# The expert outputs of a mixture layer go back to their tokens by indirect DMA stores in place of one-hot matmuls

## The chip, the core and the metric

The kernel runs on one core of a Trainium2 chip. The metric is the device time of one launch, in microseconds; the times given are medians over runs. Its engines are called as the profile calls them: PE (TensorE, with PEld for its weight loads), DVE (VectorE), ACT (ScalarE), POOL (GpSimd) and SP (SyncE, which here only issues DMAs). "PEq", "SPq" and so on are the sequencers of these engines.

## The reference, cut to what matters

A trunk of two layers over 256 tokens of width 1024. Only the last block matters here, an expert layer that sends each token to its two best of eight experts:

```python
top_v, top_i = lax.top_k(logits, 2)
top_w = jax.nn.softmax(top_v, axis=-1)
combine = jnp.sum(jax.nn.one_hot(top_i, 8) * top_w[..., None], axis=-2)
out = jnp.zeros_like(h)
for e in range(8):                       # w_gate[e], w_up[e]: 1024 x 3584, w_down[e]: 3584 x 1024
    out = out + combine[..., e:e + 1] * swiglu(h, w_gate[e], w_up[e], w_down[e])
x = x + g2 * out                         # then a final RMSNorm with shift and scale
```

All is float32. The eight experts' weights are 352 MB of the 500 MB that the kernel reads.

## The kernel before, in words

The work before the expert layer (retention, a dense SwiGLU, attention, the router) isn't touched. The expert layer runs from about 644 us to the end.

**Passes.** Expert e is one pass: 128 slots hold the tokens that chose it (a ninth to eleventh pass would serve experts with over 128 tokens; in the profiled run there are 8 passes, numbered 0 to 7 here). A pass has 7 chunks of 512 hidden columns, and a chunk has 6 units of weights of 1 MB: two of gate, two of up, two of down. Pass 0 and the last chunk of pass 7 are written out; passes 1 to 7 run in a hardware loop (`Fori`, L2050 on PE), whose body first ends pass w-1 (its last chunk and its last down step), and begins pass w. That stretch is called the turn from one pass to the next.

**One unit.** SP waits until PE has used up the slot of the ring (6 slots, semaphore `w_used`, L412) and loads 1 MB in two DMAs (L416). ACT casts it to the high part (`high_e`, L906), DVE subtracts to get the low part (`low_e`, L1432, two operands in SBUF: `stage` and `hi`), and PE multiplies three times, high by high, high by low and low by high (`three`, L1656 to L1658): 12 matmuls of 128x128 by 128x512 a unit. The order of the work on each engine is written out by hand; each engine runs ahead of PE as far as the ring allows.

**Tokens of a pass.** DVE builds one-hot matrices of slots by comparing a row of indices with each token's position (`choose`, L1477): `pick` for the pass whose output is to be put back, `pick_next` for the next pass. PE turns `pick` by two transposes (L1968) and multiplies `pick_next` by the token numbers, which gives the token of each slot of the next pass (L1970). ACT copies both out (`take_put`, L940). POOL makes an integer of the token numbers (L603) and fetches these rows of the hidden state by an indirect DMA into `grow` (L607). Some 80 us later PE transposes `grow` (L1978), for the next pass.

**Output of a pass.** The down product of pass w-1 lies in PSUM banks 4 and 5. ACT copies its high part (`take_down`, L954), DVE makes the low part (`low_down`, L1520), and PE scatters the 128 slots back to 256 tokens by 8 matmuls with the turned `pick`:

```python
def scatter(n):
    pe.wait_ge(dn_done, n)
    pe.wait_ge(put_done, n)
    for t in range(TT):
        for n in range(2):
            cols = slice(n * CB, (n + 1) * CB)
            mm(bank[:, (6, 4)[t] + n, :], put[:, t * P:(t + 1) * P], dn_hi[:, cols], start=True, stop=False)
            ins = mm(bank[:, (6, 4)[t] + n, :], put[:, t * P:(t + 1) * P], dn_lo[:, cols], start=False, stop=True)
        ins.then_inc(scat, 1)
```

DVE adds the result, weighted, to the sum `moe` (`add`, L1528, twice a pass). PE's first down step of pass w waits for that (L2064), since it writes banks 4 and 5 again.

**The end.** After the last unit, `take_down`, `low_down` and `scatter` run once more for the last pass (L2073), DVE adds it to the residual (L1621, L1625), and the final norm and the store of the output follow.

Of the kernel before, what the change touches and what calls it, by code (L numbers as in the profile page):

```python
# [8 lines left out]
P = 128  # L9
D = 1024  # L10
SEQ = 256
# [9 lines left out]
E = 8  # L21
# [33 lines left out]
SLOTS = 128  # L55
N_TAB = 16
# [25 lines left out]
def shape_constants():  # L82
# [16 lines left out]
    c[:, C_EPS + 1:C_EPS + 1 + TT] = np.arange(SEQ).reshape(TT, P).T  # L99
    j = np.arange(P)[:, None]  # L100
# [9 lines left out]
def encoder(nc, x, c, l0_ada_w, l0_ada_b, l0_norm1_g, l0_norm2_g, l0_ret_w_in, l0_ret_decay_logit,  # L110
# [5 lines left out]
    with ctx:  # L116
# [95 lines left out]
        gidx = at("gidx", [1], R + 52 * KW, I32)  # L212
        grow = at("grow", [D], R + 16 * KW)
        eaT2_hi = at("eaT2_hi", [4, SLOTS], R + 20 * KW, F32R)
# [22 lines left out]
        h_dram = nc.dram_tensor("h_rows", [SEQ, D], F32, kind="Internal").ap()  # L237

# [122 lines left out]
        grow_free = sem("grow_free")  # L361

# [36 lines left out]
        def _(sp):  # L399
# [6 lines left out]
            sp.sem_inc(moe_add, TT)  # L406
            sp.sem_inc(scat, 1)
# [113 lines left out]
        def _(pool):  # L521
# [77 lines left out]
            passes = pool.value_load(meta[0:1, 2 * N_TAB:2 * N_TAB + 1], min_val=E, max_val=E + 3)  # L599
            with pool.Fori(1, passes) as w:  # L600
# [4 lines left out]
                pool.wait_ge(g_tr, w)  # L605
                pool.sem_inc(grow_free, 1)
                nc.gpsimd.indirect_dma_start(out=grow[:, :], out_offset=None, in_=h_dram[:, :],  # L607
                                             in_offset=bass.IndirectOffsetOnAxis(ap=gidx[:, 0:1].bitcast(U32), axis=0)
                                             ).then_inc(grow_in, 16)


        @block.scalar
        def _(act):
# [322 lines left out]
            def take_put(w, first=False):  # L936
                act.wait_ge(put_tr, w + 1)
                if not first:
                    act.wait_ge(gidx_done, w)
                nc.scalar.copy(put[:, 0:SEQ + 1], bank[:, 3, 0:SEQ + 1]).then_inc(put_done, 1)  # L940
# [35 lines left out]
            take_put(0, True)  # L976
# [5 lines left out]
            with act.Fori(1, passes) as w:  # L982
# [15 lines left out]
                take_down(w, m + (RING + U_MOE + 4))  # L998
# [4 lines left out]
                take_put(w)  # L1003
# [5 lines left out]
            high_e(U_END - 1, m, o)  # L1009
            e_high_act(o + (E * N_EC - 1), eaT2_hi)  # L1010
            take_down(extra + E, m + (RING + U_END))
# [1086 lines left out]
```

## Time and profile before

| what | value |
|---|---|
| median of 3 runs (lowest, highest) | 1654.36 us (1654.05, 1655.42) |
| the profiled execution's own time | 1656.82 us |
| its span | 1654.6 us |
| PE busy | 1563.3 us, 94% of the span |
| DVE busy | 1362.7 us, 82% |
| ACT busy | 978.9 us, 59% |
| POOL busy | 151.7 us, 9% |
| moved by DMA | 503.16 MB |

The busy time of an engine is the union of its instructions' times. Matmuls overlap each other in the records: one is listed with 0.40 us, but the next starts 0.23 us after it, and it is this distance that counts. All times "at x us" are from the start of the span.

### The profile page before, as it was taken

How to read it: one execution, taken by the hardware profiler on the slowest of the kernel's cores; microseconds unless marked ns; L12 is line 12 of the kernel's file. 1: busy time of each engine (PE TensorE's matmuls, PEld its weight loads, DVE VectorE, ACT ScalarE, POOL GpSimd, SP SyncE). 2: the span in 40 equal slices, each digit the busy share in tenths (PEclk: the TensorE clock that was granted, in tenths of full speed). 3: DMA queues.
4: the chain of work that ended last, by engine and by line, in shares of the span. 5: the costliest groups of instructions: out<-in, count | busy, mean ns of one | idle time of the engine just before them, and what ended most of it. 6: DMA issues, size and time to landing. Idle time of an engine off the chain costs nothing.

```text
span 1654.6 us, 20642 instructions
## 1 busy us (share of the span) xinstructions
PE 1563.3 (94%) x6848; PEld 1248.5 (75%) x6848; DVE 1362.7 (82%) x1076; ACT 978.9 (59%) x790; POOL 151.7 (9%) x146
## 2 busy tenths in 40 slices
PE   5999779899997689999999999999999999999996
PEld 4677547677776568887888888888888888888885
DVE  6799478877767767888888888888888888888987
ACT  3444523433433636677777677677667667677763
POOL 0399400000002001000000000000000000000000
PEclk8999989999998898999999999999999999999998
DMA  9799319698894325999999999999999999999993
GB/s 340 281 346 354 118 38 360 234 304 268 296 323 131 121 67 203 378 365 347 357 368 353 356 366 353 356 369 352 356 367 353 356 367 353 355 366 355 343 368 119
DMA packets 237789, 503.16 MB, mean 304 GB/s; under 512 B 15725, under 2 KB 38381, under 8 KB 237625
## 3 DMA queue, kind: packets, MB, share of 16 engines
q1 hardware_dynamic: 234704, 491.50, 82.8%
q0 software_dynamic: 2464, 9.09, 1.6%
q10 hardware_dynamic: 586, 2.11, 0.3%
q8 instruction: 21, 0.34, 0.1%
q14 instruction: 14, 0.11, 0.0%
HBM read 500.54 MB, written 2.11 MB: 304 GB/s over the span
## 4 chain that ended last, share of the span: by engine, by line
PE 90%; DVE 6%; ACT 1%; issue 1%; DMA 1%; SPq 0%; DVEq 0%; ACTq 0%
PE bank L1656 27%; PE bank L1657 27%; PE bank L1658 27%; PE bank L1984 1%; PE bank L1637 1%; PE bank L1746 1%; DVE lo L1032 1%; DMA xs<-in_x 1%; PE bank L1651 0%; DVE hs L1070 0%; PE bank L1642 0%; PE bank L1864 0%; PE bank L2008 0%; SPq L435 0%; PE bank L2007 0%
## 5 line engine op out<-in xcount | busy, mean ns | idle before, releaser
L1432 DVE TENSOR_TENSOR lo<-stage,hi 128x2048 fp32r<-128x2048 f32 x168 | 383.7, 2287 | 53.0 <-ACT hi L906 52.7
L906 ACT CAST hi<-stage 128x2048 fp32r<-128x2048 f32 x168 | 321.4, 1913 | 134.0 <-DMA stage<-in_l_moe_w_up 119.0
L1657 PE MATMUL bank<-lo,hg_hi 128*128 128x512 f32 x896 | 354.3, 395 | 0.0
L625 ACT CAST hi<-stage 128x2048 fp32r<-128x2048 f32 x75 | 143.2, 1912 | 146.9 <-PE bank L1658 75.0
L1032 DVE TENSOR_TENSOR lo<-stage,hi 128x2048 fp32r<-128x2048 f32 x75 | 173.2, 2312 | 42.0 <-ACT hi L625 35.7
L1657 PEld LDWEIGHTS bank<-lo,hg_hi 128*128 128x128 f32 x896 | 168.8, 188 | 37.6
L1656 PE MATMUL bank<-hi,hT_hi 128*128 128x512 f32 x416 | 172.8, 415 | 10.0 <-DVE lo L1032 8.5
L1656 PE MATMUL bank<-hi,hg_hi 128*128 128x512 f32 x452 | 180.0, 398 | 0.2 <-issue 0.2
L1658 PE MATMUL bank<-hi,hg_lo 128*128 128x512 f32 x452 | 179.0, 396 | 0.0
L1657 PE MATMUL bank<-lo,eaT_hi 128*128 128x512 f32 x448 | 177.7, 397 | 0.0
L1657 PE MATMUL bank<-lo,hT_hi 128*128 128x512 f32 x416 | 167.5, 403 | 0.0
L1658 PE MATMUL bank<-hi,hT_lo 128*128 128x512 f32 x416 | 167.3, 402 | 0.0
L1432 DVE TENSOR_TENSOR lo<-stage,hi_h 128x2048 fp32r<-128x2048 f32 x56 | 128.3, 2291 | 40.2 <-ACT hi_h L906 40.0
L906 ACT CAST hi_r<-stage 128x2048 fp32r<-128x2048 f32 x56 | 106.9, 1908 | 61.1 <-DMA stage<-in_l_moe_w_gate 59.7
L1044 DVE SCALAR_TENSOR_TENSOR ada_acc<-ada_w,cact,ada_acc 128x512 f32<-128x512 f32 x168 | 131.8, 785 | 7.4 <-DVE ada_acc L1044 2.3
L1432 DVE TENSOR_TENSOR lo<-stage,hi_m 128x2048 fp32r<-128x2048 f32 x56 | 128.2, 2290 | 10.4 <-ACT hi_m L906 10.0
L1432 DVE TENSOR_TENSOR lo<-stage,hi_r 128x2048 fp32r<-128x2048 f32 x56 | 128.1, 2288 | 9.2 <-ACT hi_r L906 8.5
L906 ACT CAST hi_h<-stage 128x2048 fp32r<-128x2048 f32 x56 | 107.1, 1912 | 41.1 <-DMA stage<-in_l_moe_w_gate 40.7
L906 ACT CAST hi_m<-stage 128x2048 fp32r<-128x2048 f32 x56 | 107.2, 1914 | 40.3 <-DMA stage<-in_l_moe_w_down 40.3
L1656 PEld LDWEIGHTS bank<-hi,hT_hi 128*128 128x128 f32 x416 | 80.3, 193 | 32.5 <-DVE lo L1032 6.4
L1658 PEld LDWEIGHTS bank<-hi,hg_lo 128*128 128x128 f32 x452 | 85.1, 188 | 20.9
L1656 PEld LDWEIGHTS bank<-hi,hg_hi 128*128 128x128 f32 x452 | 85.1, 188 | 20.7 <-issue 0.4
(291 smaller groups left out, 2703.2 us busy)
## 6 DMA issues: line engine op xcount, KB each, us to landing
stage<-in_l_moe_w_gate SPq DMA_DIRECT2D x224, 512.0 KB, 4.5
stage<-in_l_moe_w_up SPq DMA_DIRECT2D x224, 512.0 KB, 4.9
stage<-in_l_moe_w_down SPq DMA_DIRECT2D x224, 512.0 KB, 4.5
ada_w<-in_l_ada_w SPq DMA_DIRECT2D x40, 1024.0 KB, 5.3
stage<-in_l_ret_w_in SPq DMA_DIRECT2D x48, 512.0 KB, 7.5
stage<-in_l_ffn_w_gate SPq DMA_DIRECT2D x22, 512.0 KB, 7.6
stage<-in_l_ffn_w_up SPq DMA_DIRECT2D x22, 512.0 KB, 8.6
stage<-in_l_ffn_w_down SPq DMA_DIRECT2D x22, 512.0 KB, 7.6
```

The lines of the kernel that those rows point to most:

```text
L625: nc.scalar.copy(hi[:, b % HRING, :], stage[:, b % RING, :]).then_inc(hi_done, 1)
L906: nc.scalar.copy(hi_e(b), stage[:, b % RING, :]).then_inc(hi_done, 1)
L1032: nc.vector.tensor_tensor(lo[:, b % RING, :], stage[:, b % RING, :], hi[:, b % HRING, :].bitcast(F32), ALU.subtract).then_inc(lo_done, 1)
L1044: ins = nc.vector.scalar_tensor_tensor(out=acc, in0=ada_w[:, half, j, :], scalar=cact[:, k:k + 1], in1=acc if k else ada_b[:, :], op0=ALU. ...
L1432: nc.vector.tensor_tensor(lo[:, b % RING, :], stage[:, b % RING, :], hi_e(b).bitcast(F32), ALU.subtract).then_inc(lo_done, 1)
L1637: mm(bank[:, 3, :], ones, ada_acc[:, c % 2, :], start=True, stop=True).then_inc(a_sum, 1)
L1656: mm(dst_ap, a_hi, w_hi, start=first, stop=False)
L1657: mm(dst_ap, a_hi, w_lo, start=False, stop=False)
L1658: return mm(dst_ap, a_lo, w_hi, start=False, stop=last)
L1746: ins = mm(bank[:, (7, 2)[t], :], dec[:, h % 2, jt * SEQ + t * P:jt * SEQ + (t + 1) * P], proj[:, 4 + h, jt, :], start=(jt == 0), stop=(jt ...
L1984: ins = nc.tensor.transpose(bank[:, 2, k * P:(k + 1) * P], eact[:, k * P:(k + 1) * P], ident)
```

## The change

Every pass but the last no longer scatters by matmuls. ACT copies the down product once, at full width, into `yout`; POOL stores its 128 rows by an indirect DMA to an internal DRAM tensor `y_rows` of 512 rows: row n is token n's result from its first expert, row 256 + n that from its second. Slots without a token get an index over the bound and are skipped. The rows are set to zero first (two DMAs of 1 MB from the zeroed `moe`). The index of each row comes from a matmul of the one-hot matrix with a table `tokv` of 9 columns (`index_rows`), which takes the place of the transposes and of the one-column product. After the last turn POOL reads `y_rows` back (four DMAs of 512 KB), multiplies both halves by their weights and adds them into `moe`; DVE's last stretch waits for that. The last pass still scatters by matmuls. The diff, cut to its core (new semaphores and their declarations are left out):

```diff
+        y_dram = nc.dram_tensor("y_rows", [2 * SEQ, D], F32, kind="Internal").ap()
...
             nc.gpsimd.memset(moe[:, :, :], 0.0).then_inc(m_zero, 1)
+            yv = y_dram.rearrange("(r t p) d -> r p t d", r=2, p=P)
+            pool.wait_ge(m_zero, 1)
+            for r in range(2):
+                pool.dma_start(yv[r], moe[:, :, :]).then_inc(y_zero, 16)
...
             with pool.Fori(1, passes) as w:
+                e = pool.value_load(meta[0:1, bass.ds(w, 1)], min_val=0, max_val=E - 1)
                 pool.wait_ge(put_done, w)
+                pool.wait_ge(sidx_done, w)
                 pool.sem_inc(put_seen, 1)
-                nc.gpsimd.tensor_copy(gidx[:, 0:1], put[:, SEQ:SEQ + 1].bitcast(F32)).then_inc(gidx_done, 1)
+                nc.gpsimd.tensor_copy(snext[:, 0:1], ix[:, bass.ds(e, 1)]).then_inc(snext_done, 1)
+                nc.gpsimd.tensor_copy(gidx[:, 0:1], ix[:, 8:9]).then_inc(gidx_done, 1)
...
                 nc.gpsimd.indirect_dma_start(out=grow[:, :], out_offset=None, in_=h_dram[:, :],
...
+                nc.gpsimd.tensor_scalar(snext[:, 0:1], snext[:, 0:1], float(NOWHERE), None, ALU.add).then_inc(snext_done, 1)
+                pool.wait_ge(dn_out, w)
+                pool.sem_inc(y_go, 1)
+                nc.gpsimd.indirect_dma_start(out=y_dram[:, :],
+                                             out_offset=bass.IndirectOffsetOnAxis(ap=sidx[:, 0:1].bitcast(U32), axis=0),
+                                             in_=yout[:, :], in_offset=None, bounds_check=2 * SEQ - 1, oob_is_err=False
+                                             ).then_inc(y_out, 16)
+                pool.wait_ge(y_out, w * 16)
+                pool.wait_ge(snext_done, w * 2)
+                pool.sem_inc(y_sent, 1)
+                nc.gpsimd.tensor_copy(sidx[:, 0:1], snext[:, 0:1]).then_inc(sidx_done, 1)
...
+            for t in range(TT):
+                pool.dma_start(moe[:, t, :], yv[0, :, t, :]).then_inc(y_in, 16)
+                pool.dma_start(ysec[t][:, :], yv[1, :, t, :]).then_inc(y_in, 16)
+            pool.wait_ge(y_in, 64)
+            for t in range(TT):
+                nc.gpsimd.tensor_scalar(moe[:, t, :], moe[:, t, :], rsm[:, t, 5, 2:3], None, ALU.mult)
+                link(nc.gpsimd.tensor_scalar(ysec[t][:, :], ysec[t][:, :], rsm[:, t, 5, 3:4], None, ALU.mult))
+                nc.gpsimd.tensor_tensor(moe[:, t, :], moe[:, t, :], ysec[t][:, :], ALU.add).then_inc(y_sum, 1)
...
+            def take_out(w, used):
+                act.wait_ge(w_used, used)
+                act.wait_ge(y_sent, w)
+                nc.scalar.copy(yout[:, :], bank[:, 4:6, :].rearrange("p b n -> p (b n)")).then_inc(dn_out, 1)
...
-                take_down(w, m + (RING + U_MOE + 4))
+                take_out(w, m + (RING + U_MOE + 4))
...
+            act.wait_ge(put_tr, extra + (E + 1))
+            nc.scalar.copy(put[:, 0:SEQ], bank[:, 3, 0:SEQ]).then_inc(put_done, 1)
...
             choose(pick_next, slice(1, 2)).then_inc(pick_done, 1)
+            for t in range(TT):
+                nc.vector.tensor_copy(tokv[:, t, 8:9], cst[:, C_EPS + 1 + t:C_EPS + 2 + t])
+                ins = nc.vector.tensor_scalar(tokv[:, t, 0:E], rsm[:, t, 7, :], float(SEQ), cst[:, C_EPS + 3 + t:C_EPS + 4 + t],
+                                              ALU.mult, ALU.add)
+            ins.then_inc(tokv_done, 1)
...
-                choose(pick, bass.ds(col, 1))
                 choose(pick_next, bass.ds(col_next, 1)).then_inc(pick_done, 1)
...
-                low_down(w)
                 low_e(b + 3, m)
                 e_low_act(o)
-                add((w * TT, w * TT + 1), bass.ds(before, 1))
...
+            def index_rows(w):
+                pe.wait_ge(pick_done, w + 2)
+                for t in range(TT):
+                    ins = mm(bank[:, 3, 0:9], pick_next[:, t, :].bitcast(F32), tokv[:, t, 0:9], start=(t == 0), stop=(t == TT - 1))
+                ins.then_inc(put_tr, 1)
...
                 e_half(U_MOE + 4, 0, m)
-                scatter(w)
-                turn_pick(w)
                 e_half(U_MOE + 4, 1, m)
-                pe.wait_ge(moe_add, w * TT + TT)
+                pe.wait_ge(put_done, w)
+                index_rows(w)
+                pe.wait_ge(dn_out, w)
                 e_down_step(U_MOE + 8, m, o, True, False)
...
+            pe.wait_ge(put_done, extra + E)
+            turn_pick(extra + (E + 2))
             e_gate_up(U_END - 8, m, o + (E * N_EC - 1))
...
-            scatter(passes)
+            scatter()
```

`yout` takes the place of `dn_hi` in SBUF, and the second halves are read into `grow` and `normg`. DVE's last stretch (L1610) waits for `y_sum` in place of `moe_add`, and makes the last `pick` there.

## Rows read from the trace of the kernel before

**Rows 1.** The page, part 2: busy tenths of PE in forty slices of the span
```profile
PE   5999779899997689999999999999999999999996
```

**Rows 2.** Window of one pass: from:to, each engine's busy us (instructions), granted clock, DMA share, GB/s
```profile
888.00:1012.00 124.00, 124.00 (x554) 100.41 (x553) 108.49 (x65) 88.74 (x60) 2.78 (x2) 1.00 0.98 359
```

**Rows 3.** Waits of PE in 657 to 1636 us; then of SP's queue: us, times, longest
```profile
PE bank L1656 <- issue: 0.5, 1, 0.5
...
SPq L416 <- PE bank L1658: 737.6, 359, 42.5
```

**Rows 4.** Timeline of PE at the first turn: start us, us, instruction (lines left out repeat the pattern)
```profile
785.01 0.40 PE L2007 MATMUL bank<-dn_hi,put 128*128 128x512 f32 x1
...
786.86 0.38 PE L1968 MATMUL bank<-cst,pick 128*128 128x128 f32 x2
787.08 0.50 PE L1970 MATMUL bank<-cst,pick_next 128*128 128x1 f32 x4
787.44 0.47 PE L1656 MATMUL bank<-hi,hg_hi 128*128 128x512 f32 x1
```

**Rows 5.** The tile `moe`: instructions, ns min/median/max, first and last start
```profile
L1528 DVE SCALAR_TENSOR_TENSOR moe<-bank,comb,moe x14: 1272/1276/1285, 786.5 to 1532.8; 128x1024 f32<-128x1024 f32 x14
```

**Rows 6.** Timelines of DVE and PE: when a unit's low part is made, and its first matmul, twice
```profile
701.78 2.29 DVE L1432 TENSOR_TENSOR lo<-stage,hi_h 128x2048 fp32r<-128x2048 f32 x1 [0.86 <-ACT hi_h L906]
708.62 0.48 PE L1656 MATMUL bank<-hi_h,hg_hi 128*128 128x512 f32 x1
788.84 2.28 DVE L1432 TENSOR_TENSOR lo<-stage,hi 128x2048 fp32r<-128x2048 f32 x1
793.14 0.39 PE L1656 MATMUL bank<-hi,eaT_hi 128*128 128x512 f32 x1
```

**Rows 7.** Windows right after a gather, columns as in rows 2
```profile
664.00:684.00 20.00, 20.00 (x90) 16.11 (x89) 17.60 (x10) 12.77 (x9) 0.00 (x0) 1.00 1.04 392
664.00:704.00 40.00, 40.00 (x177) 32.27 (x176) 35.77 (x20) 27.84 (x18) 0.00 (x0) 1.00 1.03 380
```

**Rows 8.** POOL's gather: the line, its landing, and the transposes that use it (first and last start)
```profile
L607 POOL DMA_INDIRECT grow<-h_rows,gidx x7: 1014/2592/2593, 659.5 to 1410.3; - x7
...
DMA to landing us min/median/max: 6.0/8.0/8.0
...
L1978 PE MATMUL bank<-cst,grow x56: 272/272/273, 743.2 to 1490.2; 128*128 128x128 f32 x56
```

**Rows 9.** Timelines of POOL and DVE at 200 us, then L1032 in 210 to 500 us
```profile
200.74 1.71 POOL L564 TENSOR_TENSOR proj<-proj,gn 128x512 f32<-128x512 f32 x1
201.25 3.35 DVE L1032 TENSOR_TENSOR lo<-stage,hi 128x2048 fp32r<-128x2048 f32 x1
L1032 DVE TENSOR_TENSOR lo<-stage,hi x40: 2279/2292/2295, 213.1 to 496.1; 128x2048 fp32r<-128x2048 f32 x40
```

**Rows 10.** POOL's elementwise work by line: ns min/median/max
```profile
L564 POOL TENSOR_TENSOR proj<-proj,gn x8: 1263/1372/3314, 196.2 to 208.1; 128x512 f32<-128x512 f32 x8
L596 POOL MEMSET moe<- x1: 1805/1805/1805, 630.6 to 630.6; 128x2048 f32 x1
```

**Rows 11.** The layer's start: a window (columns as in rows 2), then timelines of DVE and PE
```profile
633.00:647.00 14.00, 13.80 (x82) 13.10 (x81) 8.78 (x13) 7.99 (x6) 0.00 (x0) 0.77 0.00 1
655.65 0.69 DVE L1487 TENSOR_TENSOR eact<-bank,esil 128x512 f32<-128x512 f32 x1 [0.27 <-PE bank L1658]
656.39 0.66 PE L1984 MATMUL bank<-cst,eact 128*128 128x128 f32 x4 [0.23 <-DVE eact L1487]
```

**Rows 12.** The end: timelines of ACT, then of PE
```profile
1628.27 0.59 ACT L949 CAST eaT_hi<-bank 128x512 fp32r<-128x512 f32 x1 [2.00 <-PE bank L1984]
1639.09 0.51 PE L2007 MATMUL bank<-dn_hi,put 128*128 128x512 f32 x1 [2.43 <-DVE dn_lo L1520]
1639.66 0.62 PE L2007 MATMUL bank<-dn_hi,put 128*128 128x512 f32 x1
1640.08 0.63 PE L2008 MATMUL bank<-dn_lo,put 128*128 128x512 f32 x1
```

More of the change, by code:

```diff
@@ L55 @@
 SLOTS = 128
+NOWHERE = 4096
 N_TAB = 16
@@ L212, in encoder @@
         gidx = at("gidx", [1], R + 52 * KW, I32)
+        sidx = at("sidx", [1], R + 52 * KW + 8, I32)
+        snext = at("snext", [1], R + 52 * KW + 16)
+        ix = at("ix", [32], R + 52 * KW + 32)
+        tokv = at("tokv", [TT, 16], R + 52 * KW + 64)
+        yout = at("yout", [D], R + 42 * KW)
         grow = at("grow", [D], R + 16 * KW)
+        ysec = [grow, normg]
         eaT2_hi = at("eaT2_hi", [4, SLOTS], R + 20 * KW, F32R)
@@ L361, in encoder @@
         grow_free = sem("grow_free")
+        y_zero = sem("y_zero")
+        y_out = sem("y_out")
+        y_sent = sem("y_sent")
+        y_go = sem("y_go")
+        y_in = sem("y_in")
+        y_sum = sem("y_sum")
+        dn_out = sem("dn_out")
+        snext_done = sem("snext_done")
+        sidx_done = sem("sidx_done")
+        tokv_done = sem("tokv_done")
         def in_unit(u):
@@ L405, in _ @@
             sp.sem_inc(proj_out, 3)
-            sp.sem_inc(moe_add, TT)
-            sp.sem_inc(scat, 1)
+            sp.sem_inc(y_sent, 1)
             sp.sem_inc(g_tr, 1)
@@ L934, in take_rows, with take_index @@
                 nc.scalar.copy(hg_hi[:, :, :], bank[:, 6:8, :].rearrange("p b (k n) -> p (b k) n", k=4)).then_inc(hg_hi_done, 1)
-            def take_put(w, first=False):
+            def take_index(w, first=False):
                 act.wait_ge(put_tr, w + 1)
-                if not first:
+                if first:
+                    nc.scalar.copy(ix[:, 0:24], bank[:, 3, 0:24]).then_inc(put_done, 1)
+                else:
                     act.wait_ge(gidx_done, w)
-                nc.scalar.copy(put[:, 0:SEQ + 1], bank[:, 3, 0:SEQ + 1]).then_inc(put_done, 1)
+                    act.wait_ge(snext_done, w * 2)
+                    nc.scalar.copy(ix[:, 0:9], bank[:, 3, 0:9]).then_inc(put_done, 1)
             def e_silu_step(n, used):
@@ L975, in _ @@
             e_high_act(0)
-            take_put(0, True)
+            take_index(0, True)
             high_e(U_MOE + 8)
@@ L1009, in _ @@
             high_e(U_END - 1, m, o)
+            act.wait_ge(put_tr, extra + (E + 1))
+            nc.scalar.copy(put[:, 0:SEQ], bank[:, 3, 0:SEQ]).then_inc(put_done, 1)
             e_high_act(o + (E * N_EC - 1), eaT2_hi)
+            act.wait_ge(y_sent, extra + E)
             take_down(extra + E, m + (RING + U_END))
@@ L1609, in _ @@
             m = mods[:, 1, 2]
-            dve.wait_ge(moe_add, passes * TT)
             for t in range(TT):
+                dve.wait_ge(y_sum, t + 1)
                 ins = nc.vector.tensor_tensor(moe[:, t, :], moe[:, t, :], m, ALU.mult)
@@ L1998, in e_down_step, with scatter @@
                         e_turn(between)
-            def scatter(n):
-                pe.wait_ge(dn_done, n)
-                pe.wait_ge(put_done, n)
+            def scatter():
+                pe.wait_ge(dn_done, 1)
+                pe.wait_ge(put_done, extra + (E + 1))
                 for t in range(TT):
@@ L2041, in _ @@
             e_half(U_MOE, 1, 0)
-            turn_pick(0)
+            pe.wait_ge(tokv_done, 1)
+            for t in range(TT):
+                mm(bank[:, 3, 16:24], pick[:, t, :].bitcast(F32), tokv[:, t, 0:E], start=(t == 0), stop=(t == TT - 1))
+            index_rows(0)
             e_turn(0)
```

39 lines of the change are left out of this document (20 added, 19 removed).

## The prediction

> **What bounds the kernel now.** I read the slices first. The last 24 of 40 show PE at 9 tenths nearly throughout [rows 1]: the expert layer. A window as long as a pass then says PE 124.00 us of 124.00, DVE 108.5, ACT 88.7, DMA share 0.98 at 359 GB/s [rows 2]. So two resources are nearly full, PE and the DMA, and the waits must say which one leads. PE waits 0.5 us in the whole layer, while SP's queue waits 737.6 us for PE to free a slot of the ring [rows 3]. PE leads: what it sheds is gained, as long as weights, ACT and DVE keep up. How far they are ahead is in rows 6. A low part is done at 701.78 + 2.29 = 704.07 us and used at 708.62, a lead of 4.5 us; after a turn, where DVE has extra work, it is 793.14 - 791.12 = 2.0 us.
>
> One turn lies between the first adds at 786.5 and the next; the last add starts at 1532.8, some 1.2 us after its pair's first, so six turns take 745.1 us, 124.2 us each [rows 5].
>
> **Part 1, PE in the turns.** The scatter starts at 785.01 us, the transposes at 786.86, the one-column product at 787.08, the next gate matmul at 787.44 [rows 4]: 2.43 us. What stays is a product of 9 columns in place of one, two instructions of the same kind; no row has 9 columns, so I bound it by 0.36 us (one column, 787.44 - 787.08) and 0.6 us (with the 0.22 us that two 128-column transposes take on top). I take 0.36, as 9 columns are nearest to one. The saving is 2.07 us a turn, on the path since PE never waits; seven turns give **14.5 us** (12.8 at the other bound). A pass becomes 122.1 us.
>
> **Part 2, DVE and ACT in the turns.** DVE loses two adds of 1.28 us [rows 5], a low part of half a unit's width (half of the 2.28 us in rows 6) and one pair of comparisons, some 4 us; ACT copies 9 columns instead of 257. No PE wait ends on either now, so this is 0 us; it only lifts the lead above its low of 2.0 us.
>
> **Part 3, the stores and the gather.** A store is 128 rows of 4 KB at most, 0.52 MB, about half of it on average (512 results over 8 experts are 64 rows each). The nearest row is the gather of the same size: 2.6 us on POOL, landing in at most 8 us [rows 8]. POOL now holds the gather back until the store has landed: issued near 785 us, landed near 795, gather issued near 797 and landed near 805. The first gather, issued at 659.5 us, is used at 743.2 [rows 8]; 42 us before the scatter of its turn (785.01). With turns 124.2 us apart the next rows are wanted at about 867 us, so 60 us are left. `yout` is wanted again a pass later. ACT's wait for `y_sent`, behind which its casts are queued, costs nothing for the same reason. On the DMA the cost is bytes: 42 units of 1.049 MB and a gather make 44.6 MB a pass now (359 GB/s over 124.2 us, as rows 2 have it), 44.8 to 45.1 MB then, over 122.1 us: 367 to 369 GB/s. After the first gather the DMA moved 392 GB/s for 20 us and 380 for 40 us with PE never idle [rows 7]. So the weights can keep up: 0 us; if they can't, that is the second rival.
>
> **Part 4, the start.** The zeros are 2.1 MB, sent from about 633 us. From 633 to 647 us the DMA moves 1 GB/s, since the ring is full [rows 11]; at 392 GB/s they need 5.4 us. Hidden. DVE makes `tokv` by four operations on at most 8 columns before its `eact` at 655.65 us, where it had 0.27 us to spare, and PE already waits for that [rows 11]. No row shows so narrow a one; each costs more than nothing and less than the 0.69 us of `eact` with 512 columns. I take 0.14 us each, near the low end as they are narrow: 0.55 - 0.27 = **0.3 us** (0 to 2.5).
>
> **Part 5, reading back.** After turn 7 (about 1520 us) POOL loads 2.1 MB beside the weights: 5.4 us of the DMA at 392 GB/s. Against it stands the lead of 4.5 us [rows 6].
>
> Then POOL combines: four scalings and two additions of 128x1024. This is where I expect a loss. At 200.74 us POOL starts a tensor_tensor that reads SBUF; DVE's subtraction at 201.25, in the very shape of the expert layer, takes 3.35 us where 40 others take 2.29 [rows 9]. The 1.06 us extra are the rest of POOL's operation (it ends at 202.45), and POOL's longest operation there, 3.31 us against a least of 1.26 [rows 10], is the reverse. So such operations exclude each other, and DVE, 87% busy mostly with these subtractions, alternates with POOL. A POOL addition of 512 columns takes 1.26 us, so 1024 take about 2.35 (double is 2.53, of which I take off a little, since part of the 1.26 is a fixed cost). A scaling isn't in the trace: the memset writes 2048 columns in 1.81 us [rows 10], 0.9 us for 1024, the lower end; 2.35 us is the upper end. I take 1.0, since with one input it is nearest to the memset. The sum held against DVE is 4 x 1.0 + 2 x 2.35 = 8.7 us, less the 12.5% that DVE idles [rows 2] over some 25 us, 3 us: 5.7 us. Readback and combine together are 5.4 + 5.7 = 11.1 us late; if they share one lead of 4.5 us, PE stops 6.6 us; if the lead is won back between them, 0.9 + 1.2 = 2.1 us. I take the middle, **4.4 us**. The ends of this term: 0, if DVE's idle time and its lifted lead cover all, and 12 us, with scalings of 2.35 us (14.1 us held) and a clock that falls while PE starves.
>
> The Trainium skill (SBUF — State Buffer, Who interferes with whom) says that a DVE instruction with two SBUF inputs contends with a GpSimd instruction that reads SBUF, and that the second to issue fully blocks. Rows 9 agree, by 3.35 against 2.29 us.
>
> **Part 6, the end.** Two transposes before the last chunk: **0.2 us**. ACT's copy of `put`, shorter than the 0.59 us of 512 columns, falls into the 2.00 us that it idles before 1628 us [rows 12]. DVE's wait for `y_sum` stands at that point too, and is met some 60 us early. The last scatter and the norm don't change.
>
> **Sum.** -14.5 + 0.3 + 4.4 + 0.2 = **-9.6 us**. The profiled execution took 1656.8 us (1654.6 us of span and 2.2 around it) and would take 1647.2. The runs' median is 2.5 us lower, 1654.4, so I predict **1644.8 us** there, with a range of its own of 1642 to 1648.
>
> **The rivals.**
> *The lead covers the combine.* No stall: -14.5 + 0.5 = -14.0, 1640.4 us. For it: DVE is relieved of some 4 us just before. Against it: 11 us of disturbance lie within some 30. Chance 0.15.
>
> *The DMA is the bound (slower).* Were 359 GB/s [rows 2] what the DMA can hold on average, a pass with its store would take 45.1 MB / 359 = 125.6 us instead of 124.2, seven of them +9.8 us, and the readback 2.1 MB / 359 = 5.8 us more: +15.6, 1670 us. It decides below 369 GB/s, and loses outright below 363 (45.1 MB in 124.2 us). For it: every pass shows 359. Against it: the queue waits for PE [rows 3], and 392 and 380 GB/s were moved in rows 7. Chance 0.06.
>
> The Trainium skill (DMA: Bandwidth & Descriptors, Specifications) gives a limit from device memory of about 358 GB/s for a core; by that rule this rival would be right. Rows 7 exceed it by a tenth. The same skill (HBM Reference, Specifications (TRN2)) has a core that streams alone at about 425 GB/s, which rows 7 do not contradict.
>
> *The combine starves PE.* Scalings as slow as additions, or a reading back that is slower than its bytes: -14.5 + 0.5 + 11 = -3, 1651.4 us. After an idle of 2.43 us PE's matmuls follow each other at 0.42 us (1639.66 to 1640.08) instead of 0.23 [rows 12], so stalls of that length cost again until the clock is back. Chance 0.13.
>
> *It does not do what it says.* If a store, with its check of the bound, took over 70 us, the gather would be late and each turn would wait. At 8 us for the gather this is far off. Chance 0.02, about no change.
>
> **How the numbers follow.** The forecast has 0.64. A measurement of this kernel can tell 0.2%, 3.3 us, from no change: faster means under 1651.1, slower over 1657.7. Faster: 0.64 + 0.15, nearly half of the third rival, and those runs of the DMA case that only eat a part: 0.87. Same: 0.07. Slower: 0.06. The range takes in the first rival and most of the third: 1639.5 to 1651.
>
> **What would show it.** Right: PE's timeline at 785 us goes from gate to up matmuls without a gap, and two matmuls of 128x9 stand before the down step; turns 122.1 us apart; PE idle 2 to 7 us in all between 1520 and 1560 us, put down to DVE's low parts, with subtractions of 3 to 4.5 us beside POOL's scalings. Each scaling near 1.0 us. DMA at 367 to 369 GB/s in a pass. Wrong: PE waiting for DVE or DMA in every turn (the DMA bound), turns over 123 us apart, or POOL's gather issued more than 40 us after the store.

## The result and the profile after

Side by side on one chip, the changed kernel takes 1643.93 us (median of 5 runs, 1642.87 to 1647.75) and the kernel before 1655.42 us (5 runs, 1654.05 to 1656.88). The ratio is 0.9936, with a 95% interval of 0.9922 to 0.9950. That is 0.6% and clear of no change, so faster by the bound of 0.2% that the forecast set. I had forecast 1644.8 us, and faster with 0.87.

The page of the profiled execution (1642.87 us, span 1641.0 us), parts 1 and 2:

```profile
PE 1545.9 (94%) x6782; PEld 1234.3 (75%) x6782; DVE 1341.8 (82%) x1047; ACT 976.7 (60%) x791; POOL 198.3 (12%) x189
POOL 0399500000002001100100100000000000000600
```

PE's slices in the expert layer are at 9 tenths, as in [rows 1]. POOL's last busy slice, a 6 that is third from the end, is the combination of the results.

**The turn.** The timeline of PE at the first turn, to be read against [rows 4]:

```profile
787.29 0.39 PE L1715 MATMUL bank<-hi,hg_lo 128*128 128x512 f32 x1
787.52 0.51 PE L2025 MATMUL bank<-tokv,pick_next 128*128 128x9 f32 x4
787.88 0.48 PE L1713 MATMUL bank<-hi,eaT_hi 128*128 128x512 f32 x1
```

The scatter and the transposes are gone. The product of 9 columns takes 787.88 - 787.52 = 0.36 us, the value taken for it.

**A pass.** A window of the length of a pass, columns as in [rows 2]:

```profile
888.00:1010.00 122.00, 122.00 (x545) 98.86 (x544) 104.78 (x60) 88.83 (x60) 4.74 (x6) 1.00 1.00 367
```

PE is busy all the time, and the DMA delivers 367 GB/s where it delivered 359 [rows 2].

**The waits** of 640 to 1500 us in the trace after (us, times, longest), then PE's of 1515 to 1625 us:

```profile
POOL sidx L650 <- DMA y_rows<-yout,sidx: 28.7, 6, 5.1
ACT ix L995 <- PE bank L2025: 23.0, 6, 4.6
...
PE bank L1713 <- DVE lo L1496: 2.5, 2, 1.3
```

The second line is new. ACT copies the indices of the next pass (`ix`), and since the change these come from the product that stands behind the two up units. ACT waits 2.6 to 4.6 us for it at every turn, with its casts of weights queued behind. The last line is the only wait of PE between 1515 and 1625 us.

**Where the time went.** The layer has 42 units a pass, 336 in all, numbered from 0. The time of PE's first matmul of a unit cuts the span into stretches. "Lead" is the time from the end of a unit's low part on DVE to its first matmul, as in [rows 6].

| stretch | before | after | difference |
|---|---|---|---|
| start to the first expert matmul | 644.12 | 641.18 | -2.9 |
| to unit 295, in the last pass (six turns) | 871.80 | 859.21 | -12.6 |
| unit 295 to 335 (seventh turn, reading back) | 117.77 | 119.70 | +1.9 |
| unit 335 to the end | 20.89 | 20.89 | 0.0 |
| sum (span) | 1654.6 | 1641.0 | -13.6 |

The first row isn't the change's. It is TensorE's clock while the router is computed. The windows of before, then of after (granted clock third from the end):

```profile
627.00:644.00 17.00, 16.92 (x107) 16.73 (x107) 9.37 (x27) 11.63 (x10) 1.80 (x1) 0.70 0.26 101
```

```profile
627.00:641.00 14.00, 13.98 (x109) 13.74 (x108) 9.51 (x27) 11.76 (x10) 3.23 (x3) 0.88 0.73 281
```

PE does about the same work at a mean of 0.70 there and of 0.88 here. Over the runs of the changed kernel and its variants the first expert matmul lies between 638.4 and 644.3 us, so this is scatter (e3_no_readback, which starts the layer at 644.26, shows the slow clock there as well). It is also why single spans are compared by stretches below. The change's own part is -12.6 + 1.9 = -10.7 us.

A turn saves 2.07 us: from a unit to the same unit of the next pass it is 124.23 us before and 122.15 after, the difference before rounding 2.07. Six turns make -12.4 of the second row, and the first turn saved 0.2 more. In the third row the seventh turn's -2.07 and the 0.2 of the pick ahead of the last chunk would leave -1.9; it shows +1.9, so the stall behind the seventh turn is **+3.8 us**. The experiments are about that stall.

**The stall in the trace.** POOL after the last store, in the trace after:

```profile
1513.11 1.48 POOL L643 DMA_INDIRECT y_rows<-yout,sidx  x1 [109.68 <-ACT yout L1015]
1518.90 0.21 POOL L650 CAST sidx<-snext 128x1 int32<-128x1 f32 x1 [4.31 <-DMA y_rows<-yout,sidx]
1519.61 0.58 POOL L655 DMA_DIRECT2D moe<-y_rows  x1 [0.51 <-issue]
...
1521.26 0.54 POOL L656 DMA_DIRECT2D normg<-y_rows  x1
1532.25 2.87 POOL L659 TENSOR_SCALAR moe<-moe,rsm 128x1024 f32<-128x1024 f32 x1 [10.45 <-DMA normg<-y_rows]
1535.10 4.25 POOL L660 TENSOR_SCALAR grow<-grow,rsm 128x1024 f32<-128x1024 f32 x1
1539.43 2.58 POOL L661 TENSOR_TENSOR moe<-moe,grow 128x1024 f32<-128x1024 f32 x1
1542.00 7.00 POOL L659 TENSOR_SCALAR moe<-moe,rsm 128x1024 f32<-128x1024 f32 x1
1548.98 5.27 POOL L660 TENSOR_SCALAR normg<-normg,rsm 128x1024 f32<-128x1024 f32 x1
1554.33 2.58 POOL L661 TENSOR_TENSOR moe<-moe,normg 128x1024 f32<-128x1024 f32 x1
```

DVE beside it, same trace:

```profile
1534.34 2.29 DVE L1496 TENSOR_TENSOR lo<-stage,hi 128x2048 fp32r<-128x2048 f32 x1 [3.83 <-ACT hi L958]
1537.14 2.61 DVE L1496 TENSOR_TENSOR lo<-stage,hi 128x2048 fp32r<-128x2048 f32 x1
1539.67 4.49 DVE L1496 TENSOR_TENSOR lo<-stage,hi_m 128x2048 fp32r<-128x2048 f32 x1
...
1546.89 2.52 DVE L1496 TENSOR_TENSOR lo<-stage,hi_r 128x2048 fp32r<-128x2048 f32 x1
1549.33 5.32 DVE L1496 TENSOR_TENSOR lo<-stage,hi 128x2048 fp32r<-128x2048 f32 x2
1555.17 3.89 DVE L1496 TENSOR_TENSOR lo<-stage,hi 128x2048 fp32r<-128x2048 f32 x1
```

And ACT, then PE, where the two disturbances reach them:

```profile
1521.09 0.17 ACT L995 COPY ix<-bank 128x9 f32<-128x9 f32 x1 [4.13 <-PE bank L2025]
1532.39 1.91 ACT L958 CAST hi<-stage 128x2048 fp32r<-128x2048 f32 x1 [5.61 <-DMA stage<-in_l_moe_w_up]
```

```profile
1536.68 0.50 PE L1713 MATMUL bank<-hi,hg_hi 128*128 128x512 f32 x1 [1.18 <-DVE lo L1496]
1544.21 0.50 PE L1713 MATMUL bank<-hi_m,eaT_hi 128*128 128x512 f32 x1 [1.34 <-DVE lo L1496]
```

The reader sees two stalls with two causes. The reads go out in one burst at 1519.6 us, and the next up unit reaches ACT 5.61 us after ACT is free for it; PE stops at unit 307. Then the subtraction at 1539.67 takes 4.49 us, with POOL's first addition (1539.43 to 1542.01) ahead of it; PE stops at unit 309. The two waits listed are 2.5 us of the 3.8. Set unit by unit against a trace without the stall (e3 below), PE is later by 1.34 us at unit 307, 0.31 at 308, 1.60 at 309, and 0.5 in all at 310, 314 and 315, in gaps too short for the list of waits.

### The profile page after: what moved, and what is told of

Its sections match the earlier page's. It is cut to its first block, busy times and chain, and to the rows that moved or that the text cites. A ratio compares the mean times of both kernels' runs of the same rounds, so it can differ in the third digit from the quotient of the medians.

```text
span 1641.0 us, 20506 instructions
## 1 busy us (share of the span) xinstructions
PE 1545.9 (94%) x6782; PEld 1234.3 (75%) x6782; DVE 1341.8 (82%) x1047; ACT 976.7 (60%) x791; POOL 198.3 (12%) x189
## 4 chain that ended last, share of the span: by engine, by line
PE 89%; DVE 6%; ACT 1%; DMA 1%; issue 1%; SPq 0%; DVEq 0%; ACTq 0%
PE bank L1713 27%; PE bank L1714 27%; PE bank L1715 27%; PE bank L2045 1%; PE bank L1694 1%; PE bank L1803 1%; DVE lo L1096 1%; DMA xs<-in_x 1%; DMA stage<-in_l_moe_w_up 1%; PE bank L1708 1%; DVE hs L1134 0%; PE bank L1921 0%; DVE lo L1496 0%; SPq L453 0%; PE bank L2039 0%
## 5 line engine op out<-in xcount | busy, mean ns | idle before, releaser
L643 POOL DMA_INDIRECT y_rows<-yout,sidx x7 | 10.3, 1469 | 774.1 <-ACT yout L1015 774.1
```

## The experiments

Theory A: the lead is used up by ACT's new wait, by the bytes read back, and by POOL's arithmetic, which keeps DVE off. Theory B: the extra DMA traffic alone makes the stall. Theory C: the DMA is the bound throughout. The column "295 to 335" is taken from the profiled execution of each; the change without any disturbance shows 115.92 there. Each is one trace, and the stop at unit 307 alone, read against e3, lies between 0.9 and 1.5 us over seven traces that read back in one burst (e5, e2, e6, after_again, e1, the changed kernel, e8; 2.0 in after_third), so differences of half a microsecond between stretches say little.

| run | 295 to 335, us | last pass's least lead | median us | ratio to before, 95% |
|---|---|---|---|---|
| changed kernel | 119.70 | 0.05 | 1643.93 | 0.9936 [0.9922, 0.9950] |
| e1_index_early | 119.74 | 0.05 | 1644.09 | 0.9946 [0.9930, 0.9961] |
| e2_no_combine | 117.11 | 0.05 | 1641.91 | 0.9923 [0.9909, 0.9938] |
| e3_no_readback | 115.92 | 1.37 | 1638.78 | 0.9908 [0.9892, 0.9924] |
| e4_store_twice | 120.25 | 0.05 | 1645.39 | 0.9951 [0.9936, 0.9966] |
| e5_scale_more | 118.80 | 0.05 | 1642.42 | 0.9927 [0.9914, 0.9941] |
| e6_act_combine | 117.47 | 0.06 | 1642.09 | 0.9920 [0.9902, 0.9937] |
| e8_act_scale | 117.79 | 0.06 | 1645.67 | 0.9947 [0.9930, 0.9963] |
| after_again | 119.70 | 0.06 | 1642.83 | 0.9935 [0.9920, 0.9950] |
| e9_paced_act | 117.43 | 1.05 | 1641.07 | 0.9920 [0.9907, 0.9934] |
| e10_paced_pool | 119.74 | 0.06 | 1646.29 | 0.9946 [0.9932, 0.9959] |
| after_third | 122.66 | 0.05 | 1644.18 | 0.9935 [0.9921, 0.9948] |
| e11_paced_early | 115.93 | 1.07 | 1640.95 | 0.9920 [0.9902, 0.9938] |

The expectations speak of unit 300 to 335. Where the index product is early, it falls ahead of unit 300 and not behind it, which shortens that stretch by some 0.3 us (105.25 becomes 104.92 in e1) and gains nothing; from unit 295 on the columns compare.

**e1_index_early.** PE makes the index product before the second half.

```
+                pe.wait_ge(put_done, w)
+                index_rows(w)
                 e_half(U_MOE + 4, 1, m)
-                pe.wait_ge(put_done, w)
-                index_rows(w)
                 pe.wait_ge(dn_out, w)
```

> Edit: PE makes the index rows between the two halves of the chunk, where the turned one-hot matrix was made before, and no longer after the second half. Theory A (ACT's copy of the index waits some 4 us for PE at each turn, and this eats the lead of DVE over PE, so that at the last turn the reading back and the combine find a lead of 1.4 us): ACT's wait before its copy of ix falls from 27 us in all to under 3, the least lead at the turns rises from 1.4 us to 2.5 or more, and PE's stall after the last turn falls from 3.8 us to 1 to 2, so the time falls by 2 to 3 us against the changed kernel (some 1641.5). Rival B (the low lead comes from the store's bytes on the DMA, not from ACT's wait): the wait goes, the leads stay under 2 us, the stall and the time stay within 1 us.

ACT's wait for `ix` vanished from the list of waits, and the least leads behind the first six turns rose from 1.37 to between 1.85 and 3.05 us, so rival B's leads under 2 us came at one turn of the six. The stall did not fall either, as theory A had it: the stretch is 119.74. The timeline of ACT in this run:

```profile
1517.26 0.16 ACT L995 COPY ix<-bank 128x9 f32<-128x9 f32 x1
1524.69 1.91 ACT L958 CAST hi<-stage 128x2048 fp32r<-128x2048 f32 x1 [0.85 <-DMA stage<-in_l_moe_w_up]
1532.61 1.91 ACT L958 CAST hi<-stage 128x2048 fp32r<-128x2048 f32 x1 [6.00 <-DMA stage<-in_l_moe_w_up]
```

ACT is no longer late, but the unit behind the reads is still cast at 1532.61 (1532.39 in the changed kernel), which is 31.98 us behind unit 295 here and 32.00 there. Its landing is set by the DMA, whatever ACT did before. So the new wait is real and costs nothing here: this step of theory A falls.

**e2_no_combine** leaves out the weighting and adding of the stored results (they are read back), **e3_no_readback** the reading back as well.

```
-            for t in range(TT):
-                nc.gpsimd.tensor_scalar(moe[:, t, :], moe[:, t, :], rsm[:, t, 5, 2:3], None, ALU.mult)
...
+            pool.sem_inc(y_sum, TT)
```

> Edit: POOL's four scalings and two additions at the end are left out (so the experts' outputs are not weighted and the second halves are not added), the reading back stays. Theory A (POOL's operations and DVE's subtractions exclude each other): DVE's subtractions after the last turn are all 2.29 us long, and PE's stall there falls from 3.8 us to under 1.5; the time is 2.5 to 4 us under that of the changed kernel, some 1640. Rival B (the stall is the DMA's, by the 2.1 MB read back): the stall stays at 3 us or more.

> Edit: neither reading back nor combine (the outputs of all experts but the last are left out of the result). Both theories: no stall of PE in the expert layer, turns 122.1 us apart, and the floor of this design: the span's part from the first expert matmul to the end is 3.8 us shorter than in the changed kernel, about 1640. Against the run without the combine it prices the reading back alone: theory A 0 to 1.5 us, rival B 3 us or more.

Without the arithmetic the stretch is 117.11, without the reads 115.92. So the reads alone cost 117.11 - 115.92 = **1.2 us**, and the arithmetic on top of them 119.70 - 117.11 = **2.6 us** (0.2 of it at unit 307, where no subtraction was long yet). No subtraction is long in e2, as expected; its median is 2.0 us under the changed kernel's, where 2.5 to 4 were expected. ACT in e3 at the unit that stands behind the reads in the others:

```profile
1530.56 1.91 ACT L951 CAST hi<-stage 128x2048 fp32r<-128x2048 f32 x1 [0.75 <-DMA stage<-in_l_moe_w_up]
```

Counted from unit 295 (at 1500.39 us in the changed kernel, 1503.41 in e3), this cast starts at 32.00 and at 27.15: the burst makes it 4.9 us late. PE came 1.34 us late for it, so 3.5 us were covered: 2.6 by the lead at unit 307 (2.63 in e3), and 0.9 because DVE took the cast up at once instead of 1.0 us later.

**e4_store_twice** stores the rows of every pass a second time, to another DRAM tensor.

```
+                nc.gpsimd.indirect_dma_start(out=y_more[:, :],
+                                             out_offset=bass.IndirectOffsetOnAxis(ap=sidx[:, 0:1].bitcast(U32), axis=0),
+                                             in_=yout[:, :], in_offset=None, bounds_check=2 * SEQ - 1, oob_is_err=False
+                                             ).then_inc(y_out, 16)
```

> Edit: each pass stores its rows twice, the second time into another DRAM tensor, and POOL waits for both (no output changes). Theory A (PE paces the layer and the DMA has room): turns stay 122.1 us apart, the gather is issued 1.5 to 3 us later and still some 50 us early, the time is that of the changed kernel within 1.5 us. Rival C (the DMA is the bound, at 359 to 369 GB/s): 0.26 to 0.5 MB more a pass make turns 0.7 to 1.4 us longer, 5 to 10 us in all, some 1650 to 1654.

The turns stay at 122.15 us; only the last pass takes 0.55 us more. Theory C falls: the DMA still has room for another store in every pass. Counted from the first expert matmul POOL issued the gather 4.2 us later than in the changed kernel (1.5 to 3 were expected); its rows are used at 865.9 us, and no wait of PE came of it:

```profile
784.66 2.79 POOL L648 DMA_INDIRECT y_more<-yout,sidx  x1 [0.30 <-issue]
794.20 1.27 POOL L655 CAST sidx<-snext 128x1 int32<-128x1 f32 x1 [6.76 <-DMA y_more<-yout,sidx]
796.92 2.19 POOL L638 DMA_INDIRECT grow<-h_rows,gidx  x1 [0.91 <-POOL gidx L633]
```

**e5_scale_more** makes each scaling twice, so the combination uses the squares of the weights.

```
+                for _ in range(2):
+                    link(nc.gpsimd.tensor_scalar(moe[:, t, :], moe[:, t, :], rsm[:, t, 5, 2:3], None, ALU.mult))
+                    link(nc.gpsimd.tensor_scalar(ysec[t][:, :], ysec[t][:, :], rsm[:, t, 5, 3:4], None, ALU.mult))
```

> Edit: every scaling of the read-back results on POOL is made twice (so each result is multiplied by its weight squared), the additions stand as they are. Theory A (POOL's arithmetic holds DVE off and lengthens its subtractions, and the last lead is already gone when it starts): six long POOL instructions become ten, the stretch from unit 300 to 335 grows from 105.2 us by 1.5 to 4 us, more than five subtractions are long, time 1645.5 to 1648. Theory B (the stall is made by the DMAs of the reading back, not by arithmetic): the stretch stays at 105.2 within 0.4 us and the time at 1644. A third way, that only the additions exclude DVE (two inputs) and the scalings do not: no change either, but the scalings' own rows would then last 1 us each when no subtraction runs.

None of the three came. Twice the scalings made the stall *shorter*, 118.80 against 119.70. Half of the difference, 0.45 us, stands at unit 307 (PE 0.89 us late instead of 1.34), where no subtraction is long in either trace, so that half comes from the reads and not from the scalings. The rows of POOL bear on the other half, and on why nothing grew:

```profile
1539.66 5.14 POOL L660 TENSOR_SCALAR moe<-moe,rsm 128x1024 f32<-128x1024 f32 x1
1544.89 3.04 POOL L661 TENSOR_SCALAR grow<-grow,rsm 128x1024 f32<-128x1024 f32 x1
1548.02 2.60 POOL L662 TENSOR_TENSOR moe<-moe,grow 128x1024 f32<-128x1024 f32 x1
```

The addition now comes 8.6 us later (1548.02, against 1539.43), and hits the low part of unit 312, when the lead is 1.1 us, instead of that of unit 309, when it is 0.06. Summing what DVE's subtractions take over 2.29 us each: in the changed kernel 5.2 us, (the row of two counts as 5.32 less 4.49, what two take unhindered), of which the two subtractions behind additions have 2.20 (4.49) and 1.60 (3.89), and all that run beside four scalings 1.4. In e5 it is 7.2 us: again 3.8 for the additions, and 3.4 for eight scalings. So an addition holds a subtraction that starts beside it for what is left of the addition, less 0.14 us (2.20 us of 2.34, 1.60 of 1.74), and a scaling holds DVE for about 0.4 us. It is the scaling that yields: it takes 2.87 us at its shortest and 7.00 where DVE subtracts without a pause (1542.00 to 1549.00).

**e6_act_combine** keeps the index product early, and moves the scalings to ACT behind its last cast and the additions to DVE in front of its work at the end. **e8_act_scale** leaves the additions on POOL.

```
+            act.wait_ge(y_in, 64)
+            for t in range(TT):
+                nc.scalar.mul(moe[:, t, :], moe[:, t, :], rsm[:, t, 5, 2:3])
+                nc.scalar.mul(ysec[t][:, :], ysec[t][:, :], rsm[:, t, 5, 3:4]).then_inc(y_sum, 1)
             act.wait_ge(y_sent, extra + E)
...
                 dve.wait_ge(y_sum, t + 1)
+                link(nc.vector.tensor_tensor(moe[:, t, :], moe[:, t, :], ysec[t][:, :], ALU.add))
```

> Edit: the index product of the next pass stands before the second half again, the four scalings of the results read back move from POOL to ACT behind its last cast of the last expert, where ACT idled 7.8 us, and the two additions to DVE in front of the multiplication by the final factor, where DVE idled 4.3 us. POOL does no arithmetic there. Theory A (2.6 us of the 3.8 us stall is POOL's arithmetic, the rest the bytes of the reading back): the stretch from unit 300 to 335 falls from 105.2 to 102.3 to 102.7, no subtraction after 1500 us is long, the end from unit 335 stays at 20.9 within 0.5 us, time 1640.5 to 1642. Rival (the end is then set by ACT's scalings and DVE's additions, 4.2 and 2.5 us): the end grows by 2 to 3 us and the time stays at 1644.

> Edit: as the run with the scalings on ACT, but the two additions stay on POOL, behind the scalings, where DVE does its last few instructions. Theory A: by then no weight's low part is left for DVE, so the stretch from unit 300 to 335 is 102.3 to 102.7 here too; what the additions cost is at the end, where DVE waits for the second of them (2.6 us each, after ACT's last scaling some 4.2 us behind its last cast): the end from unit 335 grows by 0 to 2.5 us, time 1641 to 1643.5. Theory B, that the DMAs make the stall: the stretch stays near 105.

In e6 no subtraction is long, the stretch is 117.47 (102.65 from unit 300) and the end stays at 20.88 us: the rival falls. ACT's scalings and DVE's additions, in e6:

```profile
1617.83 1.14 ACT L1072 ACTIVATE normg<-normg,rsm 128x1024 f32<-128x1024 f32 x1
1622.62 1.01 ACT L1004 CAST dn_hi<-bank 128x1024 fp32r<-128x1024 f32 x1 [3.65 <-PE bank L1715]
```

```profile
1620.70 1.23 DVE L1668 TENSOR_TENSOR moe<-moe,normg 128x1024 f32<-128x1024 f32 x1
1623.73 1.23 DVE L1583 TENSOR_TENSOR dn_lo<-bank,dn_hi 128x1024 fp32r<-128x1024 f32 x1 [0.54 <-ACT dn_hi L1004]
```

A scaling takes 1.14 us on ACT and an addition 1.23 on DVE; both still idle before the last down result. In e8 the stretch is 117.79 (102.97 from unit 300, where 102.7 was the most expected; its stop at unit 307 is 0.3 us longer than e6's). But the end grew by 4.0 us, to 24.9, more than the 0 to 2.5 that I gave it, and the median missed its range too (1645.67). DVE waited 5.48 us for POOL, and then its multiplication was held by POOL's second addition; POOL, then DVE:

```profile
1620.42 2.36 POOL L659 TENSOR_TENSOR moe<-moe,normg 128x1024 f32<-128x1024 f32 x1
```

```profile
1620.49 3.37 DVE L1671 TENSOR_TENSOR moe<-moe,mods 128x1024 f32<-128x1024 f32 x1 [5.48 <-POOL moe L659]
```

3.37 us where the same line takes 1.22 alone; the 2.15 us extra are again what was left of POOL's addition (2.29 us, to 1622.78) less 0.14.

**after_again**, the changed kernel as it is.

> The changed kernel as it is, for a comparison on the same chip and in the same call. All theories: 300 to 335 at 105.2 us, turns 122.15 us, time 1643 to 1645, and the same least leads at the turns (1.4 us), the last near 0.

The stretch repeats to the hundredth, 119.70.

**e9_paced_act** is e6 with the four reads four units apart, from 24 units before the end on. **e10_paced_pool** has them three apart from 26 on, with the arithmetic on POOL. **e11_paced_early** is e9 with the numbers (33, 27) and (30, 24): three apart, from unit 303 on.

```
             for t in range(TT):
+                pool.wait_ge(w_used, extra * UNITS_ITEM + (RING + U_END - (24, 16)[t]))
+                pool.sem_inc(y_pace, 1)
                 pool.dma_start(moe[:, t, :], yv[0, :, t, :]).then_inc(y_in, 16)
+                pool.wait_ge(w_used, extra * UNITS_ITEM + (RING + U_END - (20, 12)[t]))
+                pool.sem_inc(y_pace, 1)
                 pool.dma_start(ysec[t][:, :], yv[1, :, t, :]).then_inc(y_in, 16)
```

> Edit: as the run with ACT's scalings and DVE's additions, and the four reads of the rows (0.5 MB each) no longer stand in one burst behind the last store: each waits for a unit of the last expert to be used up, four units (11 us) apart, from the unit 24 before the end on. Theory (the burst puts 5 us of bytes ahead of one up chunk and the lead there is smaller than that; 1.4 us at a time stays below a lead of 2.5 to 4): no unit is short of its weights, the least lead of the last pass is over 0.5 us, the stretch from unit 300 to 335 falls from 102.65 to 101.3 to 101.7 us, the end stays at 20.9, time 1640 to 1641.5, some 3.5 us below the changed kernel in the same call. Rival (the bytes cost the same wherever they stand, because the queues of weights are full and the clock of the stretch is theirs): 102.6 us or more.

> Edit: the index product early and the four reads three units apart from the unit 26 before the end on, but the arithmetic stays on POOL as in the changed kernel. Theory (a long subtraction of 4.5 us costs 2.2 us less the lead that stands there, not a price of its own): the five or more long subtractions are all still there, the lead has gone to 2.5 to 4 us when they come, so the stretch from unit 300 to 335 is 101.4 to 102.3 us and not 105.2. Rival (each long subtraction costs its excess, some 5 us in all, of which 2.6 show): 103.5 us or more. The last addition on POOL ends near 1600, before DVE needs it, so the end from unit 335 stays at 20.9; time 1640 to 1642.

> The changed kernel as it is, beside the two runs with the spaced reads in the same call. All theories: 105.25 us from unit 300 to 335, 122.15 us a turn, time 1642 to 1645.

In e9 no unit waits for its weights, as expected, and still the stretch is 117.43 against e6's 117.47 (102.61 from unit 300, where 101.3 to 101.7 were expected). The reads drew the lead down late, to 1.05 us at unit 325, and the end of the pass has other customers for it. PE's rows with a wait, in e9:

```profile
1596.31 0.43 PE L2038 MATMUL bank<-cst,pick 128*128 128x128 f32 x2 [0.23 <-issue]
1611.59 0.66 PE L2051 MATMUL bank<-cst,eact 128*128 128x128 f32 x4 [0.76 <-DVE eact L1556]
```

`eact`, the activation product that PE transposes, is made by DVE in order between low parts. When the low parts are late, so is `eact`, and PE waits for it though its next weights are there. Against e3 PE loses 0.97 us there, at unit 333. It loses 0.49 us at unit 328, at the row of 1596.31, for which the profile names no releaser. The time that the rival gave came out, by a mechanism that it did not name.

In e10 the lead was 1.8 to 2.6 us when POOL began, not the 2.5 to 4 that I had given it, since the reads had just been served; PE then stopped four times, and the stretch is 119.74. My range of 101.4 to 102.3 us was missed (104.93 from unit 300), and the median too (1646.29, not 1640 to 1642). The rival's 103.5 us or more came out. But the lead had fallen to 1.07 us at unit 324, before the first long subtraction, so the run doesn't tell the rival from the theory, which had counted on 2.5 to 4. Three of its four rows of PE:

```profile
1591.84 0.50 PE L1719 MATMUL bank<-hi,eaT_hi 128*128 128x512 f32 x1 [0.75 <-DVE lo L1502]
1598.02 0.66 PE L2051 MATMUL bank<-cst,eact 128*128 128x128 f32 x4 [0.31 <-DVE eact L1557]
...
1614.98 0.66 PE L2051 MATMUL bank<-cst,eact 128*128 128x128 f32 x4 [1.09 <-DVE eact L1557]
```

after_third, the changed kernel once more, had a profiled execution out of line with its two others: 122.66 us in the stretch, and 124.5 us from its first turn to its second, where a gate unit landed late and ACT waited 2.69 us for it. What happened in the stretch is in the trace. PE at the activation product, then a window with columns as in [rows 2], both of after_third:

```profile
1550.54 0.66 PE L2045 MATMUL bank<-cst,eact 128*128 128x128 f32 x4 [1.95 <-DVE eact L1551]
```

```profile
1552.00:1554.50 2.50, 2.50 (x8) 1.92 (x7) 2.50 (x2) 2.34 (x3) 2.50 (x2) 0.50 0.85 339
```

The unit behind the reads came later (PE waited 1.8 us at unit 307), POOL's first addition met the low part ahead of `eact`, and PE waited 1.95 us for that. Then the granted clock fell to 0.50, the lower of TensorE's two levels (1.2 GHz): from 1551.5 to 1554.9 us PE's matmuls are 0.43 us apart instead of 0.23, and unit 311 is 1.56 us late. In the changed kernel's first trace PE had waited 1.18 and 1.34 us, and a window of 1519 to 1560 us shows 1.00. Why the unit landed later is open. The median of after_third is in line.

> Edit: as the run with spaced reads and ACT's scalings, but the reads start at once, three units (8.4 us) apart from the unit 33 before the end (unit 303) on, so that the last one is out at unit 312. Theory (the lead is one stock: the reads take some 5 us from it in all, it refills by about 0.2 us a unit, and PE waits when it falls below 0, or below about 2 us where a chunk's activations stand behind low parts on DVE): the least lead is 0.5 to 2 us near unit 314, it is back over 2.5 us by unit 328, no gap of 0.5 us or more at units 328 and 333, and the stretch from unit 300 to 335 is 101.3 to 102.0 us; time 1639.5 to 1641. Rival (the bytes read back cost 1.1 to 1.2 us wherever they stand): 102.5 to 102.8 us, as in the two runs with ACT's scalings before.

The stretch is 115.93 us, that of the kernel with nothing to read back. The waits of PE between 1515 and 1625 us, and two of POOL's reads:

```profile
PE bank L2074 <- DVE dn_lo L1589: 2.5, 1, 2.5
```

```profile
1524.82 0.58 POOL L659 DMA_DIRECT2D moe<-y_rows  x1 [5.35 <-PE bank L1721]
...
1550.86 0.53 POOL L662 DMA_DIRECT2D normg<-y_rows  x1 [8.30 <-PE bank L1721]
```

The one wait left is that of the last scatter, as before [rows 12]. The lead falls to 1.07 us at unit 317, is back at 3.05 at unit 327 and 3.7 at 328, and no gap opens. The rival, that the bytes cost 1.2 us wherever they stand, falls. The median is 1640.95 us, 1.9 to 3.2 us below the three medians of the changed kernel, at least two of which were taken on another chip. The intervals of the ratios overlap, so the medians alone don't show that this version is the faster one. The stretch in the traces (3.8 us shorter, the end unchanged, no long subtraction, no unit late) is the firmer evidence. Its ratio to the kernel before is 0.9920. Whether it needs the early index product was not tried alone.

## Why the prediction was right

Part 1 was right to the hundredth: 2.07 us a turn, seven times, with 0.36 us for the nine columns.

Part 2 was wrong in its last clause, "it only lifts the lead above its low of 2.0 us". The least lead at a turn fell, from 2.2 to 1.37 us. I counted the work that ACT loses in its copy of `ix`, and not what the copy now waits for: a product that stands behind two up units. [rows 3] have the waits of PE and SP and none of ACT. The cost is 0 (e1), since PE's lead in the first six turns stays above 0 and behind the last turn the DMA decides.

Part 3 was right: DMA 367 GB/s in a pass (367 to 369 expected). The store took 1.46 us on POOL where I bounded it by the gather's 2.6; the next gather was issued at 789.8 us, earlier than my 797. The rival that the DMA is the bound falls by e4.

Part 4: 0.3 us were taken for `tokv`, and no loss was found. From the first expert matmul to unit 32, with `tokv` between them, it is 93.04 us before and 93.07 after.

Part 5 had the right sum, 3.8 us measured for 4.4 forecast (0 to 12), from parts that were partly wrong. The reading back cost 1.2 us (0.9 in my forecast where it had the lead to itself): the burst delayed a unit by 4.9 us (5.4 by bytes), and 3.5 us were covered, not 4.5: the lead of 4.5 us is that of mid-pass, and behind a turn there were 2.6. Of the arithmetic, the two additions took 2.58 us each (2.35) and held DVE for 3.8 us. Four scalings were put at 1.0 us and took 2.87 to 7.00; had they held DVE for that, the stall would have been past the 11 us of my third rival. They held it for 1.4 us in all. DVE's loss was 5.2 us (5.7 forecast). The step that failed is "such operations exclude each other", drawn from rows of tensor_tensor alone [rows 9] and used for the scaling, which has one input: it yields to DVE and hardly holds it. Two errors cancelled, the scalings' length and their effect, and that is luck; so is how near the 4.4 came, which was the middle between 2.1 and 6.6 us. The sign "subtractions of 3 to 4.5 us beside POOL's scalings" came beside the additions instead, and no scaling was near 1.0 us. The clock that falls while PE starves, part of the upper end and of the third rival, showed only in after_third, for 3.4 us. The Trainium skill (SBUF — State Buffer, Who interferes with whom) has the second instruction to issue fully blocked when DVE has two inputs from SBUF; the additions agree (4.49 us against 2.29), the scalings on the whole do not.

Part 6 was right: 0.2 us, and 20.89 us from unit 335 to the end in both.

The forecast of the median is 0.9 us above the measured one, and this small distance is partly luck: I started from 1654.4 us, and side by side the kernel before took 1655.42. The change's own 10.7 us against 9.6 forecast is made of 0.6 in part 5, 0.3 in part 4, and 0.2 at the first turn. The medians differ by 11.5; the rest lies within the scatter of the start.

## What to carry to other kernels

A lead of one engine over another is a stock that everything in a stretch draws on: late bytes, longer instructions, and small in-order work such as `eact`. A disturbance costs what it takes beyond the stock at its place, so the same reads cost 1.2 to 1.5 us in a burst (e2, e6), 1.5 us spread towards the end of a pass, where the chain wants its lead again, and nothing when spread just behind the turn.

When an operation is made cheaper by taking its operand from a later product, ask what is queued behind the wait of the engine that reads the product. In this kernel elementwise work with two inputs belonged neither on POOL beside a busy DVE nor where the lead is lowest, and ACT's 7.8 us of idle time at the end took all four scalings at 1.14 us each for nothing.

## What was unexpected about the hardware

POOL's multiplication by a column of scalars seems to have a large fixed part here. The same kind of instruction on one column, then a copy of one column, in the changed kernel (ns min/median/max):

```profile
L640 POOL TENSOR_SCALAR snext<-snext x7: 1768/1781/1853, 661.1 to 1401.7; 128x1 f32<-128x1 f32 x7
...
L631 POOL COPY snext<-ix x7: 182/183/184, 656.8 to 1399.4; 128x1 f32 x7
```

1.78 us against 0.18. Taken from the shortest 128x1024 scaling (2.87), it leaves 1.1 us for 1024 columns, near the 0.9 that the memset of [rows 10] gives; but another one-column tensor_scalar of the same kernel took 0.73 us, so what the fixed part depends on is open. POOL's two-input addition holds a two-input subtraction on DVE for what is left of it (2.20 of 2.34 us); its one-input scaling holds DVE for some 0.4 us, and takes as much as 7.00 us beside it.

An indirect store of 128 rows costs POOL 1.46 us, and POOL's next instruction waited 4.31 to 5.09 us for it to land; no wait of PE came of it.
